# First block of routed rows by fp32 one-hot products, five blocks gathered, and one expert's weights held back

## The reference

```
g    = argmax(softmax(t @ wg + bg));   idx, v = top_k(softmax(le_g), 2)
hid  = silu(t @ w_gate[e]) * (t @ w_up[e]) * comb[..., e]
out  = sum_e hid @ w_down[e]
```

## Time and profile before

| what | value |
|---|---|
| median of three runs | 471.2 us |
| the profiled execution | 470.47 us |
| its span, first to last instruction | 468.6 us |
| PE busy | 415.8 us, 89% |
| DVE, ACT, POOL busy | 52%, 25%, 7% |
| mean granted TensorE clock | 0.963 of 2.4 GHz |
| bytes moved | 154.47 MB, mean 330 GB/s |
| chain that ended last | PE 80%, DMA 6%, DVE 6%, issue 4% |

### The profile page before, as it was taken

How to read it: one execution, slowest core, us unless ns; L and a number is a source line. 1 busy time by engine, 2 the same in 40 slices (tenths; PEclk the granted TensorE clock), 3 DMA queues, 4 the chain that set the end, 5 groups by cost and what they waited for, 6 DMA issues and landing times.

```text
span 468.6 us, 7205 instructions
## 1 busy us (share of the span) xinstructions
PE 415.8 (89%) x2734; PEld 223.4 (48%) x2734; DVE 243.4 (52%) x473; ACT 114.9 (25%) x222; POOL 31.6 (7%) x41
## 2 busy tenths in 40 slices
PE   0779999999999997679999999999999999999940
PEld 0434555554644444457556545545455444465420
DVE  4563724837768675820243345344353434425997
ACT  3300167186401004132321012201111111121231
POOL 2000033045000000410000000000000000000000
PEclk9989999999999997889999999999999999999975
DMA  8999995505958899999999999999999999999403
GB/s 312 387 386 386 284 387 192 179 0 172 326 196 320 301 393 398 398 400 383 396 383 395 394 388 394 396 393 388 395 395 392 392 394 394 392 390 397 182 2 135
DMA packets 66675, 154.47 MB, mean 330 GB/s; under 512 B 3768, under 2 KB 4648, under 8 KB 66232
## 3 DMA queue, kind: packets, MB, share of 16 engines
q1 hardware_dynamic: 63776, 143.33, 82.6%
q10 hardware_dynamic: 1816, 7.06, 3.9%
q0 software_dynamic: 1024, 3.24, 2.2%
HBM read 150.45 MB, written 3.17 MB: 328 GB/s over the span
## 4 chain that ended last, share of the span: by engine, by line
PE 80%; DMA 6%; DVE 6%; issue 4%; ACT 2%; SPq 1%; POOL 0%; DVEq 0%; POOLq 0%; ACTq 0%
PE PS L1832 24%; PE PS L1624 13%; PE PS L1877 12%; PE PS L1710 9%; PE PS L1917 7%; DMA ring<-in_w_in 4%; PE PS L1562 3%; PE PS L1607 2%; DMA xg<-h_rows,cnt 2%; PE PS L1842 2%; PE PS L1795 1%; PE PS L1860 1%; PE PS L1949 1%; DVE y L1460 1%; SPq L399 1%
## 5 line engine op out<-in xcount | busy, mean ns | idle before, releaser
L1832 PE MATMUL PS<-ring,xs 128*64 128x256 f32 x1024 | 120.0, 382 | 1.9 <-issue 1.8
L1832 PEld LDWEIGHTS PS<-ring,xs 128*64 128x64 f32 x1024 | 72.4, 137 | 43.0 <-issue 11.2
L1624 PE MATMUL PS<-hT,ring 128*128 128x388 f32 x192 | 67.0, 501 | 2.9 <-DMA ring<-in_w_in 2.1
L1877 PE MATMUL PS<-ring,hTs 128*64 128x512 f32 x256 | 60.3, 599 | 1.2 <-ACT hTs L691 0.6
L1624 PEld LDWEIGHTS PS<-hT,ring 128*128 128x128 f32 x192 | 36.9, 194 | 31.3 <-issue 3.4
L1355 DVE SCALAR_TENSOR_TENSOR y<-PS,comb,y 128x1024 f32<-128x1024 f32 x39 | 49.8, 1277 | 0.6 <-PE PS L1917 0.5
L1330 DVE TENSOR_TENSOR yl<-PS,yh 128x512 fp32r<-128x512 f32 x14 | 9.7, 692 | 51.6 <-ACT yh L718 42.6
L1877 PEld LDWEIGHTS PS<-ring,hTs 128*64 128x64 f32 x256 | 17.3, 136 | 35.3 <-issue 34.3
L718 ACT CAST yh<-PS 128x512 fp32r<-128x512 f32 x12 | 7.0, 586 | 84.3 <-PE PS L1877 57.7
L1245 DVE SCALAR_TENSOR_TENSOR hid<-sg,PS 128x256 f32<-128x256 f32 x14 | 5.9, 421 | 41.8 <-PE PS L1832 41.8
L1917 PE MATMUL PS<-yh,selT 64*128 64x512 f32 x96 | 23.8, 491 | 2.6 <-issue 1.8
(11 more groups left out here) (274 smaller groups left out, 475.1 us busy)
## 6 DMA issues: line engine op xcount, KB each, us to landing
ring<-in_ex_w_gate SPq DMA_DIRECT2D x16, 2048.0 KB, 18.7
ring<-in_ex_w_up SPq DMA_DIRECT2D x16, 2048.0 KB, 17.6
ring<-in_ex_w_down SPq DMA_DIRECT2D x16, 2048.0 KB, 15.7
ring<-in_w_ada SPq DMA_DIRECT2D x12, 2048.0 KB, 13.6
ring<-in_w_in SPq DMA_DIRECT2D x3, 2048.0 KB, 20.4
ring<-in_w_out SPq DMA_DIRECT2D x2, 2048.0 KB, 17.2
rows<-row_scratch ACTq DMA_DIRECT2D x3, 1024.0 KB, 4.9
h_rows<-tts ACTq DMA_DIRECT2D x3, 512.0 KB, 6.2
```

The source lines that it names most:

```text
L1624: mm = pe.matmul(PS[:, w % 4, 0:W], wt[:, k, (w % 4) * P:(w % 4 + 1) * P], hT[:, k, :], start=(k == 0), stop=(k == KD - 1))
L1832: return pe.matmul(PS[HALF * h:HALF * (h + 1), j, 0:FE // 2], x[:, k, 0:HALF], w[:, k, h * (FE // 2):(h + 1) * (FE // 2)], start=(k == 0), ...
L1877: return pe.matmul(PS[HALF * h:HALF * (h + 1), yb, :], hTs[:, f % 2, HALF * (f // 2):HALF * (f // 2 + 1)], w[:, f, h * 512:(h + 1) * 512], ...
```

## The change

1. **Block 0 without a gather.** DVE builds `sel0`, an fp32 one-hot matrix of the first 128 slots: three `tensor_scalar` and three `scalar_tensor_tensor` over 128x128. PE multiplies the three blocks `tts[i]` by it, 8 x 3 = 24 fp32 matmuls into PSUM banks 4 and 5, which gives the transposed rows of block 0. ACT copies each bank to `xs[0]` as it is done, and after the token numbers to `xTa`, `xTb`.
2. **Five gathers.** `token_ids` and `slot_tok` cover blocks 1 to 5, in one step. POOL issues gathers 1 to 5, and clears the tails of `xTa` and `xTb` after them.
3. **PE order.** `ada_cols(5)`, the slot rows (L1810, now `slot_rows`) and `x_rows(1)` to `x_rows(3)` all stand between `project_in(0, 0)` and `project_in(0, 1)`.
4. **DVE order.** The last two `mod_out` stand behind `comb` and not in front of `x1_scale(2)`.
5. **SP.** Unit 5 waits for gather 3, the third of the five; unit 6 no longer waits for a gather.
6. **Places in SBUF.** `sel`, `iota16`, `xg` and `sel0` get other addresses.

By the order above, unit 5 is the gate matrix of the third expert (expert 2). The second expert's down matrix is unit 7, and stands behind units 5 and 6 in SP's program.

```diff
@@ SP
             for v, e, j in order:
                 if v < RING:
                     sp.wait_ge(s["p1_used"], NP1 + 1 - RING + v)
+                    if v == RING - 1:
+                        sp.wait_ge(xg_in[3], 16)
                 elif v < SLOTS:
                     sp.wait_ge(s["x1_done"], NT)
-                    sp.wait_ge(xg_in[2], 16)
@@ ACT
-                act.wait_ge(s["xg_ps"], n + 1)
-                if n == 0:
-                    act.copy(xs[0][:, :, :], PS[:, b:b + 2, :]...).then_inc(s["xs_ready"], 1)
+                if n:
+                    act.wait_ge(s["xg_ps"], n)
+                else:
+                    act.wait_ge(s["h2_out"], 16 * NT)
+                    act.wait_ge(s["x0_ps"], 1)
+                    act.copy(xs[0][:, 0:KD // 2, :], PS[:, b, :]...)
+                    act.wait_ge(s["x0_ps"], 2)
+                    act.copy(xs[0][:, KD // 2:, :], PS[:, b + 1, :]...).then_inc(s["xs_ready"], 1)
+                    act.wait_ge(s["idx_ps"], 1)
...
-            act.wait_ge(s["h2_out"], 16 * NT)
-            act.wait_ge(s["prow_ps"], 1)
-            act.copy(Prow[:, :, :], PS[:, 2:4, 0:TOK]).then_inc(s["prow_sb"], 1)
+            rows_in(0)
             act.wait_ge(s["assign_done"], 2)
             (two Exp, as before)
-            for n in range(2):
-                rows_in(n)
...
             gate_tanh(0)
-            rows_in(2)
-            rows_in(3)
+            act.wait_ge(s["prow_ps"], 1)
+            act.copy(Prow[:, :, :], PS[:, 2:4, 0:TOK]).then_inc(s["prow_sb"], 1)
+            for n in range(1, 4):
+                rows_in(n)
@@ DVE
+            for i in range(NT):
+                step(dve.tensor_scalar(sel0[:, 0, i, :], slots0, pw[:, 0, i:i + 1], None, ALU.is_equal))
+            for i in range(NT):
+                dve.wait_ge(s["dve_step"], n_step[0] - NT + 1 + i)
+                dve.scalar_tensor_tensor(out=sel0[:, 1, i, :], in0=slots0, scalar=pw[:, 1, i:i + 1],
+                                         in1=sel0[:, 0, i, :], op0=ALU.is_equal, op1=ALU.add).then_inc(s["sel0_done"], 1)
...
-            token_of_slots(0, 1)
...
-            token_of_slots(1, ST)
+            dve.wait_ge(s["idx_ps"], 1)
+            dve.tensor_scalar(slot_tok[:, 1:ST], PS[:, 2, 257:256 + ST], float(TOK // 2), None, ALU.add).then_inc(s["idx_sb"], 1)
             exponents()
-            for n in range(10, 12):
-                mod_out(n)
             x1_scale(2)
             x1_shift(2)
...
             dve.tensor_tensor(comb[:, :, :], rt[:, 3], rt[:, 4], ALU.add).then_inc(s["comb_done"], 1)
+            for n in range(10, 12):
+                mod_out(n)
@@ POOL
+            pool.wait_ge(s["idx_sb"], 1)
+            for n in range(1, ST):
+                pool.indirect_dma_start(xg[n][:, :], None, t["h2_rows"][:, :], ...).then_inc(xg_in[n], 16)
+            pool.wait_ge(s["x0_ps"], 2)
             pool.memset(xTa[:, :, NSLOT:], 0.0)
             pool.memset(xTb[:, :, NSLOT:], 0.0).then_inc(s["tail0"], 1)
@@ PE
+            pe.wait_ge(s["sel0_done"], NT)
+            for k in range(KD):
+                for i in range(NT):
+                    mm = pe.matmul(PS[:, 4 + k // 4, (k % 4) * P:(k % 4 + 1) * P], tts[i][:, k * P:(k + 1) * P],
+                                   sel0[:, 1, i, :], start=(i == 0), stop=(i == NT - 1))
+                if k % 4 == 3:
+                    mm.then_inc(s["x0_ps"], 1)
             pe.wait_ge(s["sel_done"], 1)
-            token_ids(0).then_inc(s["idx_ps"], 1)
             (token_ids 1 to 5, as before)
-            ada_cols(5)
-            (slot rows, x_rows(0), x_rows(1))
...
             project_in(0, 0)
-            x_rows(2)
-            x_rows(3)
+            ada_cols(5)
+            slot_rows()
+            for n in range(1, 4):
+                x_rows(n)
             project_in(0, 1)
```

More of the change, by code:

```diff
@@ L189, in build @@
         h2T = at("h2T", A0 + 18432, [P, KD, TOK])
-        xg = [at(f"xg{n}", A0 + 30720 + n * D * 4, [P, D]) for n in range(ST)]
+        xg = {n: at(f"xg{n}", A0 + 30720 + (n if n > 1 else 0) * D * 4, [P, D]) for n in range(1, ST)}
         B0 = A0 + 39296
@@ L195, in build @@
         assert end <= base + nc.sbuf_bytes_remaining
-        sel = at("sel", A0, [P, 2, NT, NSLOT], BF16)
+        sel = at("sel", rows0, [P, 2, NT, NSLOT], BF16)
         strow = at("strow", A0, [P, P])
+        sel0 = at("sel0", A0 + 512, [P, 2, NT, P])
         Prow = at("Prow", A0 + 9216, [P, 2, TOK])
@@ L203, in build @@
         assert 12288 + KD // 2 * XCOL * 4 <= 26624 and KD // 2 * XCOL * 4 <= 16384
-        iota16 = at("iota16", A0 + 26624, [P, NSLOT], FP16)
+        iota16 = at("iota16", A0 + 30720, [P, NSLOT], FP16)
         xs = [at("xs0", A0 + 26624, [P, KD, P]), at("xs1", A0 + 30720, [P, KD, P])]
@@ L268, in build @@
             "pos_pool selB wrem p1_used state_done st_ps st_row st_out tri_done dve_step act_step pool_step "
-            "pw_done sel_done tok_done idx_ps idx_sb prow_ps prow_sb xg_ps xg_sb tail0 lgp_ps lgp_sb wr_zero io_done comb_done "
+            "pw_done sel0_done x0_ps sel_done tok_done idx_ps idx_sb prow_ps prow_sb xg_ps xg_sb tail0 lgp_ps lgp_sb wr_zero io_done comb_done "
             "unit_used xs_ready sg_done silu_done hid_done ht_ps hts_done yh_done yl_done selA2 selT_done "
@@ L659, in rows_in @@
                 b = 4 + 2 * (n % 2)
-                act.wait_ge(s["xg_ps"], n + 1)
-                if n == 0:
-                    act.copy(xs[0][:, :, :], PS[:, b:b + 2, :].rearrange("p a (k n) -> p (a k) n", n=P)).then_inc(s["xs_ready"], 1)
+                if n:
[3 more added lines that the diff above has]
+                    act.wait_ge(s["x0_ps"], 1)
+                    act.copy(xs[0][:, 0:KD // 2, :], PS[:, b, :].rearrange("p (k n) -> p k n", n=P))
+                    act.wait_ge(s["x0_ps"], 2)
+                    act.copy(xs[0][:, KD // 2:, :], PS[:, b + 1, :].rearrange("p (k n) -> p k n", n=P)).then_inc(s["xs_ready"], 1)
+                    act.wait_ge(s["idx_ps"], 1)
                 act.copy(xTa[:, :, n * P:(n + 1) * P], PS[:, b, :].rearrange("p (k n) -> p k n", n=P))
                 act.copy(xTb[:, :, n * P:(n + 1) * P], PS[:, b + 1, :].rearrange("p (k n) -> p k n", n=P)).then_inc(s["xg_sb"], 1)
-            act.wait_ge(s["h2_out"], 16 * NT)
-            act.wait_ge(s["prow_ps"], 1)
-            act.copy(Prow[:, :, :], PS[:, 2:4, 0:TOK]).then_inc(s["prow_sb"], 1)
+            rows_in(0)
             act.wait_ge(s["assign_done"], 2)
@@ L1172, in _ @@
             dve.nop().then_inc(s["pw_done"], 1)
[L1174 to L1178, removed]
+            dve.wait_ge(s["iota_in"], 16)
+            slots0 = cst[:, C_IOTA:C_IOTA + P]
+            for i in range(NT):
+                step(dve.tensor_scalar(sel0[:, 0, i, :], slots0, pw[:, 0, i:i + 1], None, ALU.is_equal))
+            for i in range(NT):
+                dve.wait_ge(s["dve_step"], n_step[0] - NT + 1 + i)
+                dve.scalar_tensor_tensor(out=sel0[:, 1, i, :], in0=slots0, scalar=pw[:, 1, i:i + 1], in1=sel0[:, 0, i, :],
+                                         op0=ALU.is_equal, op1=ALU.add).then_inc(s["sel0_done"], 1)
             dve.wait_ge(s["tok_done"], 2)
@@ L1256, in choose @@
                     dve.wait_ge(s["comb_done"], 1)
-                    dve.wait_ge(s["xg_ps"], ST)
+                    dve.wait_ge(s["xg_ps"], ST - 1)
                     dve.wait_ge(s["mod_sb"], 12)
@@ L1521, in _ @@
             pool.dma_start(t["new_state"], strow[0:2 * CR, :]).then_inc(s["st_out"], 16)
-            pool.wait_ge(s["lg_ps"], 1)
             pool.wait_ge(s["h2_out"], 16 * NT)
+            pool.wait_ge(s["idx_sb"], 1)
+            for n in range(1, ST):
+                pool.indirect_dma_start(xg[n][:, :], None, t["h2_rows"][:, :],
+                                        bass.IndirectOffsetOnAxis(ap=slot_tok[:, n:n + 1], axis=0)).then_inc(xg_in[n], 16)
+            pool.wait_ge(s["x0_ps"], 2)
             pool.memset(xTa[:, :, NSLOT:], 0.0)
             pool.memset(xTb[:, :, NSLOT:], 0.0).then_inc(s["tail0"], 1)
[L1530 to L1533, removed]
             pool.wait_ge(s["st_out"], 16)
@@ L1782, in token_ids @@
                     for i in range(NT):
-                        mm = pe.matmul(PS[:, 2 if n else 1, 256 + n:257 + n], sel[:, q, i, n * P:(n + 1) * P], tok16[:, i:i + 1],
+                        mm = pe.matmul(PS[:, 2, 256 + n:257 + n], sel[:, q, i, n * P:(n + 1) * P], tok16[:, i:i + 1],
                                        start=(q == 0 and i == 0), stop=(q == 1 and i == NT - 1))
@@ L1804, in _, with slot_rows @@
             token_ids(ST - 1).then_inc(s["idx_ps"], 1)
-            ada_cols(5)
[L1806 to L1814, removed]
+            def slot_rows():
+                pe.wait_ge(s["pw_done"], 1)
+                pe.wait_ge(s["idx_sb"], 1)
+                for q in range(2):
+                    for i in range(NT):
```

(3 more changed lines are left out.)

## The result

The changed kernel takes 476.61 us (median of four runs, 475.48 to 476.86) against 471.51 for the kernel before on the same chip: a ratio of 1.0099, 95% interval 1.0071 to 1.0127. It is 5.1 us slower. The forecast was 470.5 with a range up to 473.0. A second set on another chip gave 1.0094 (1.0061 to 1.0127).

A forecast was written before the change was run, and what follows sets the result against it. A routing latency chain and a weight stream at its limit were taken as the bounds: PE 1.6 us earlier, weights 2.7 - 2.0 = 0.7 earlier, the later deciding, so 471.2 - 0.7 = 470.5 us; range 468.9 to 473.0.

The forecast's parts named there:

- Two clocks: PE's path and the weight stream, worked out separately; the end moves by the later: PE 1.6 earlier, weights 0.7 earlier.
- a cushion of 2.7 us on the weights: At the last units, down 14 and 15 land 3.0 and 2.7 us before PE uses them, capping PE's useful gain.
- The stream is 2.0 later to the end (bounds 1.2 and 4.5): Weight stream from unit 5 on: gate 2 lands at 213.6 instead of 211.6, and the delay lasts to the end.
- Start of the gathers: POOL starts the first gather at 200.0 instead of 194.09, after the products, token numbers and `slot_tok`.
- First byte: First gathered byte 1.8 us after POOL's start on idle DMA engines, at 201.8; bounds 1.0 and 4.3.
- The gathers' bytes: Five gathers at 1.31 us each, 0.40 MB/us, take 6.55 us on the DMA engines.
- Unit 5 behind them: Gate 2's transfer takes 5.24 us after the gathers; any gap before its first byte is covered by gathers 4 and 5.
- PE's gain: `project_in(0, 0)` starts 6.1 us earlier; PE keeps 1.6 at `project_in(0, 1)`, 211.4 instead of 213.02.
- The 48 records: The 24 fp32 matmuls on PE, two records each, at 0.13 apart at the high clock: 6.2 us.
- The idle gap: Slower rival: first gathered byte 4.3 after POOL's start, at 204.3; stream 4.5 late, 1.8 slower, 473.0; chance 0.20.
- The cold products: Slower rival: the 48 records run at the lower clock, 10.5 us; stream 6.3 late, 3.6 slower, 474.8; chance 0.05.
- PE alone decides: Faster rival: the weight stream makes up its gap, PE's 1.6 or 2.3 counts, 469.6 to 468.9; chance 0.20.

The follow-up runs named there:

- the halved units: Half of units 9 to 12 not loaded: in the changed kernel 468.20 us, ratio 0.9932; in the kernel before 472.85 us, ratio 1.0018.
- the moved holds: Changed kernel, wait for gather 3 moved to unit 6: 0.9956; unit 5 held for gather 1 only: 1.0067. Kernel before, unit 5 held for gather 2: 0.9947.
- the gathers first and unit 5 held: Changed kernel with token numbers, sel and slot_tok ahead of the fp32 products, unit 5 still waiting for gather 3: 470.09 us, ratio 0.9977.
- the hold alone in the kernel before: Kernel before (six gathers, no products) with unit 5 waiting for gather 2 and unit 6 for no gather: 469.46 us, ratio 0.9947.
- the two kernels with the gathers first and unit 5 free: Changed kernel with token numbers ahead of the products: unit 6 held for gather 3, 469.10 us (0.9945); no unit held, 467.84 us (0.9934).
- with unit 6 held: Changed kernel with the wait for gather 3 moved from unit 5 to unit 6: 469.55 us, ratio 0.9956.
- the gathers first and no unit held: Changed kernel with token numbers, sel and slot_tok ahead of the products, no unit waiting for a gather: 467.84 us, ratio 0.9934.

## Why the prediction was wrong

**The frame held.** Two clocks, a cushion of 2.7 us on the weights, unit 5's landing as the joint between routing and end: the halved units and the moved holds bear them out. The cushion had been read at the last two units only. In the trace of before the smallest is the same, 2.7, there and at the down matrix that PE uses at 404.8, so that reading was sound, and that it held at the other units was luck. The change was decided by the stream, as forecast.

**The step that failed is the term "The stream is 2.0 later to the end (bounds 1.2 and 4.5)".** It was 9.0 at unit 5, and 8.2 to 8.7 at the end. By its own pieces:

- *Start of the gathers*, 200.0: measured 201.61. In this execution `ada_sums(11)` took 3.64 us for its 16 records at a granted clock of 0.50 (190.4 to 194.1), where before it took 1.92 at 1.00; so the products started at 194.03 and not 192.3. In five of the eight other traces with products it took 1.92. POOL's pick-up took 0.8 after `slot_tok`, not 0.3.
- *First byte*, 1.8 after POOL's start: measured 2.5 (204.16). It is 1.84, POOL's own first instruction, which had taken 1.05 before, and 0.7 behind its end. Over all traces this delay was 1.7 to 4.4. It was 2.5 or 2.6 in all six with the gathers behind the products, whether the engines stood idle or were full; 1.7 with the gathers first and unit 5 held; 2.7 with the hold alone in the kernel before; and 4.3 or 4.4 in both traces of the six gathers with unit 5 free and in the two kernels with the gathers first and unit 5 free.
- *The gathers' bytes*, 6.55: measured 9.5 (204.2 to 213.6, the last 1.5 shared with the start of unit 5). With the engines to themselves they moved 294 GB/s at a share of 0.90; I had taken the 400 of a full mixed queue. This term had no bound at all in my working, and its error of 2.9 is larger than the whole of my forecast shift.
- *Unit 5 behind them*, 5.24, "covered by gathers 4 and 5": measured 6.9 (213.6 to 220.6). The stream came up slowly, 330 GB/s from 212 to 218.

Together: idle 198.7 (unit 4 landed, 189.5 + 9.2) to 204.2 = 5.5, + 2.9 (gathers) + 1.7 (unit 5) - 1.3 (the gather saved) = 8.8, and unit 4 was 0.2 late: 9.0, as measured. My idle stretch was 3.3. The excess is 2.2 in the idle stretch and 4.6 in the rates behind it, and my upper bound had reckoned with a longer idle stretch only.

**PE's gain**, 1.6: in the changed kernel `project_in(0, 1)` was 0.4 earlier, and with the faster `ada_sums(11)` 2.1 (210.87 with unit 6 held). The terms of the forecast add up to 211.1 and not 211.4, which is nearer. The floor of 3.2 compares medians; between profiled executions it is less: the kernel with the gathers first and no unit held has a span 2.5 below before (466.05 and 468.55), 2.0 of it there at `project_in(0, 1)` (211.00). The rest is spread: the profiled execution of before (470.47) is 1.4 under the median of its kind on the chip of those runs, where the times go from 469.46 at a mean granted clock of 0.968 to 474.23 at 0.955. The 48 records took 5.83 at the full clock (6.2 forecast). The wait on `mod_out` stood where forecast: 0.79 us ahead of `x_rows(1)`.

**The rivals.** The idle gap was the right one, with a price that stopped at the start of the first gather. That its first byte at 204.3 was met (204.16) is luck: it had POOL at 200.0 and 4.3 behind it, and measured are 201.61 and 2.5. The cold products were right in kind but on the wrong instruction: it was the work ahead of them that ran at half clock. "PE alone decides" is true only once bytes are taken out or the gap is closed. The Trainium skill's fixed part of about 2 us ("DMA: Bandwidth & Descriptors", anatomy of a DMA on the gpsimd path) pointed to a short start, and an estimate by it is 3.2 us from issue to landing for 0.52 MB. The first gather took 5.3 on idle engines (the changed kernel with halved units), and 4.8 behind the last bytes of unit 4 (gathers first, unit 5 held). Here the measurement decides.

**What stays open:** why the gathers alone run at 294 GB/s in the changed kernel, and at 300 to 340 in the kernels with the other order or hold, when six of them ran at 367 in the kernel before with the hold moved. These kernels differ also in the places of `xg` and `sel` in SBUF (item 6 of the change) and in what the engines do meanwhile; no run separates the two. And why the first byte comes 0.7 us after POOL's first instruction in some kernels, with a full queue beside it in two of them, and over 3 us after it in others.

## What to carry to other kernels

When a stream of transfers runs at its limit to the end of the kernel, every us in which its engines stand still early on comes back at the end once a small cushion is used up; measure that cushion as use minus landing over all the late transfers, and hold it against each new gap. A wait that keeps transfers out of the way of urgent ones is good only while the urgent ones are really in flight: here the same wait was 7 us dearer on unit 5 than on unit 6 with late gathers, and gained 2.5 us on unit 5 in the kernel whose gathers went out early. Price a gap to its end: with the start, the rate of what then runs alone (here slower than the full queue), and the restart behind it.

## What the runs showed that was not expected

- A gather of 0.52 MB on idle engines took 5.3 us from issue to landing, the ones behind it in the changed kernel 5.2 to 6.5; together they moved 294 GB/s at a DMA share of 0.90. A full queue moved 392 to 400 at 1.03, and six gathers alone in the kernel before with the hold moved 367 at 0.99.
- The first indirect DMA took POOL 1.84 or 1.85 us where the gathers come behind the products, the next ones 0.93 to 0.97; with the gathers first, or in the kernel before, it took 1.03 to 1.05. The first gathered byte came 0.7 after the end of this instruction in seven of the twelve traces (the six with the late gathers, and the gathers first with unit 5 held), 1.6 after it with the hold alone in the kernel before, and 3.2 to 3.4 in the other four.
- The clock of `ada_sums(11)` differs between executions with the same work in front: 16 records in 1.92 or 3.64 us. The granted clock was 0.50 in the one and 1.00 in the other. That alone moves the routing by 1.5 to 1.7 us.
